# Causal mask folded into the bias rows, and row tiles taken from last to first

## The reference, cut to what matters

```python
s = jnp.einsum('bqhd,bkhd->bhqk', q_blk, k) * scale       # 128 query rows, 8 heads of 64
s = s + (F_blk[..., :, None] - Fh[..., None, :])          # the bias; Fh is a cumulative sum
s = jnp.where(kpos[None, :] <= qpos[:, None], s, NEG_INF) # the causal mask
p = jax.nn.softmax(s, axis=-1)
out = jnp.einsum('bhqk,bkhd->bqhd', p, v)
```

## Time and profile before

| | |
|---|---|
| median of 3 runs | 1316.46 us (1313.67 to 1316.74) |
| profiled execution | 1316.77 us |
| its span, first to last instruction | 1315.0 us |
| TensorE busy | 1287.6 us (98%) |
| VectorE / GpSimd / ScalarE busy | 698.0 / 610.7 / 401.7 us |
| mean granted TensorE clock | 0.996 |
| attention, slots 0 to 63 | from about 55.6 to 345 us |

### The profile page before, as it was taken

How to read it: one execution, slowest core, us unless ns; L and a number is a source line. 1 busy time by engine, 2 the same in 40 slices (tenths; PEclk the granted TensorE clock), 3 DMA queues, 4 the chain that set the end, 5 groups by cost and what they waited for, 6 DMA issues and landing times.

```text
span 1315.0 us, 20412 instructions
## 1 busy us (share of the span) xinstructions
PE 1287.6 (98%) x7189; PEld 1013.3 (77%) x7189; DVE 698.0 (53%) x1033; ACT 401.7 (31%) x590; POOL 610.7 (46%) x286
## 2 busy tenths in 40 slices
PE   8999999999999999999999999999999999999996
PEld 7988999998788777777777777777777777666675
DVE  5855656534657845547367473746545235312338
ACT  4646666664522241121212112020212102012016
POOL 1027878763301457475766757566662112021114
PEclk9999999999999999999999999999999999999999
DMA  7344545320362077776876868767674635577633
GB/s 246 124 152 138 171 158 175 124 89 1 128 236 78 31 232 289 245 244 230 285 254 213 270 223 273 239 229 264 236 259 155 202 129 184 219 258 270 251 118 129
DMA packets 111534, 254.96 MB, mean 194 GB/s; under 512 B 12624, under 2 KB 22737, under 8 KB 106048
## 3 DMA queue, kind: packets, MB, share of 16 engines
q1 hardware_dynamic: 66440, 181.96, 40.4%
q10 hardware_dynamic: 44032, 69.22, 15.7%
q0 software_dynamic: 960, 2.47, 0.5%
HBM read 243.72 MB, written 10.12 MB: 193 GB/s over the span
## 4 chain that ended last, share of the span: by engine, by line
PE 88%; DVE 6%; ACT 2%; issue 2%; DMA 1%; SPq 1%; POOL 0%; DVEq 0%; ACTq 0%; POOLq 0%
PE PSM L1574 35%; PE PSM L1584 16%; PE PSM L1298 12%; PE PSM L1410 5%; PE PSM L1634 4%; PE PSM L1311 3%; PE PSM L1377 3%; PE PSM L1361 2%; PE PSM L1680 2%; PE PSM L1553 1%; PE PSM L1693 1%; PE PSM L1332 1%; DVE ACC L2209 1%; DVE ACC L2228 1%; DMA QB<-q_d 1%
## 5 line engine op out<-in xcount | busy, mean ns | idle before, releaser
L893 POOL TENSOR_TENSOR WL<-WR,WH 128x1024 fp32r<-128x1024 f32 x55 | 132.0, 2400 | 379.6 <-ACT WH L1136 379.6
L801 POOL TENSOR_TENSOR AR<-AR,QB 128x1024 f32<-128x1024 f32 x96 | 238.4, 2503 | 55.0 <-DMA AR<-cache_k 52.2
L1574 PE MATMUL PSM<-XH,WH 128*128 128x512 f32 x672 | 213.5, 399 | 0.0
L1574 PE MATMUL PSM<-XL,WH 128*128 128x512 f32 x672 | 208.0, 391 | 0.0
L1574 PE MATMUL PSM<-XH,WL 128*128 128x512 f32 x672 | 207.1, 389 | 0.0
L2180 DVE TENSOR_TENSOR ACC<-ACC,PSM 128x512 f32<-128x512 f32 x160 | 108.4, 683 | 137.1 <-PE PSM L1584 136.9
L1136 ACT CAST WH<-WR 128x1024 fp32r<-128x1024 f32 x55 | 57.5, 1047 | 347.1 <-PE PSM L1574 179.4
L1574 PEld LDWEIGHTS PSM<-XH,WH 128*128 128x128 f32 x672 | 121.9, 188 | 50.4 <-issue 27.6
L1584 PE MATMUL PSM<-R 128*128 128x512 f32 x528 | 148.4, 390 | 0.1
L1574 PEld LDWEIGHTS PSM<-XH,WL 128*128 128x128 f32 x672 | 126.1, 188 | 27.4
L1574 PEld LDWEIGHTS PSM<-XL,WH 128*128 128x128 f32 x672 | 126.1, 188 | 27.3
(11 more groups left out here) (285 smaller groups left out, 2021.5 us busy)
## 6 DMA issues: line engine op xcount, KB each, us to landing
AR<-cache_v ACTq DMA_DIRECT2D x248, 256.0 KB, 4.2
AR<-cache_k SPq DMA_DIRECT2D x192, 256.0 KB, 4.0
AR<-ws SPq DMA_DIRECT2D x37, 1024.0 KB, 6.5
WR<-ffn SPq DMA_DIRECT2D x66, 512.0 KB, 4.6
WR<-w_in SPq DMA_DIRECT2D x20, 512.0 KB, 4.0
ACC<-cache_k SPq DMA_DIRECT2D x32, 256.0 KB, 2.8
WR<-cache_k SPq DMA_DIRECT2D x32, 256.0 KB, 3.1
WR<-w_o SPq DMA_DIRECT2D x5, 1024.0 KB, 5.3
```

What stands on the lines that cost most here:

```text
L801: pool.tensor_tensor(keys, keys, QB[:].rearrange("p (o n) -> p o n", o=1).to_broadcast([P, KP, AW]), ALU.mult).then_inc(k_mul, 1)
L893: pool.tensor_tensor(lo, WR[:, raw_weight(e), :], hi.bitcast(F32), ALU.subtract).then_inc(ffn_lo, 1)
L1574: ins = pe.matmul(out[:, hc], (hi, lo)[a][:, k * P:(k + 1) * P], x[b][:, k, hc], start=(k == 0 and n == 0), stop=(k == KC - 1 and n == 2))
```

## The change

The causal tile (zeros, and -1e30 above the diagonal) is no longer added by a product of TensorE in each of 64 score tiles. Instead it is added, in place, to block i of the bias row NF[hh] before row tile i is read. Block i then stays masked, and a row tile with a larger i would need it unmasked: so the row tiles of a head go from last (i = 7) to first (i = 0), by the new function `row_tile`. GpSimd adds the tile for slots 0 to 47 (`mask_block`, 48 instructions), VectorE for slots 48 to 63 (16 instructions). The addition for slot x+1 waits until VectorE has read slot x, and stands at the end of what GpSimd does in slot x; VectorE's instruction of slot x+1 waits for it (`masked`). The product steps are shared out evenly over the half slots. The mask has a tile of its own, and the rounded copies of identity and mask (two ScalarE instructions, `cons_hi`) are gone. `weighted_values` takes the tiles in their new order with the same number of products.

```diff
+POOLMASKS = STEPS * (PAIRS - 1)
+def row_tile(s):
+    return RT - 1 - s % RT
 def product_steps():
-    share = [RT + 4 - s % RT for s in range(STEPS) for _ in range(2)]
+    share = [1] * (2 * STEPS)
...
-            sp.wait_ge(cons_hi, 2)
...
+            def mask_block(x):
+                p, s = divmod(x, STEPS)
+                hh, i = s // RT, row_tile(s)
+                if s % RT == 0:
+                    pool.wait_ge(nf_ld[hh], 16 * (p + 1))
+                block = NF[hh][:, i * P:(i + 1) * P]
+                pool.tensor_tensor(block, block, causal[:], ALU.add).then_inc(masked, 1)
+                pool.wait_ge(masked, x + 1)
+
+            pool.wait_ge(small_ld, 16 * 7)
+            mask_block(0)
             for x, p, s in slots():
...
                 for n in range(EARLY):
                     if EMUL[n] == x:
                         multiply(n)
+                if x + 1 < POOLMASKS:
+                    pool.wait_ge(s_free, U["s", x] + 1)
+                    mask_block(x + 1)
...
-            act.copy(identR[:], ident[:]).then_inc(cons_hi, 1)
-            act.copy(causalR[:], causal).then_inc(cons_hi, 1)
...
             def scores(x, p, s):
-                hh, i = s // RT, s % RT
-                if i == 0:
+                hh, i = s // RT, row_tile(s)
+                if s % RT == 0:
...
                 for c in range(0, w, HALF):
                     n = min(HALF, w - c)
-                    diag = c + n == w
                     for part in (1, 2):
                         ins = pe.matmul(ps[:, c:c + n], R2[:, 3 * hh, i * P:(i + 1) * P],
-                                        R2[:, 3 * hh + part, c:c + n], start=(part == 1),
-                                        stop=(part == 2 and not diag))
-                    if diag:
-                        ins = pe.matmul(ps[:, w - P:w], identR[:], causalR[:], start=False, stop=True)
+                                        R2[:, 3 * hh + part, c:c + n], start=(part == 1), stop=(part == 2))
...
-                for kt in range(i + 2):
-                    for a in range(max(0, kt - i), 2):
+                for kt in range(i + 1):
+                    for a in range(2 if kt < i else 1):
...
                     dve.wait_ge(s_full, U["s", x] + 1)
-                    if i == 0:
-                        dve.wait_ge(nf_ld[hh], 16 * (p + 1))
+                    dve.wait_ge(masked, x + 1)
                     if x >= 2:
                         dve.wait_ge(tb_full, T["t", x - 2] + 1)
                     dve.tensor_tensor_reduce(L[x % 2][:, 0:w], S[:, 0:w], NF[hh][:, 0:w], -SCALE, 3e38,
                                              ALU.add, ALU.min, negm[:, x % 2:x % 2 + 1]).then_inc(s_free, 1)
+                if POOLMASKS <= x + 1 < SLOTS:
+                    q, r = divmod(x + 1, STEPS)
+                    dve.wait_ge(s_free, U["s", x] + 1)
+                    if r % RT == 0:
+                        dve.wait_ge(nf_ld[r // RT], 16 * (q + 1))
+                    block = NF[r // RT][:, row_tile(r) * P:(row_tile(r) + 1) * P]
+                    dve.tensor_tensor(block, block, causal[:], ALU.add).then_inc(masked, 1)
```

More of the change, by code:

```diff
@@ L249, in build @@
         ident = sb("ident_sb", [P, P])
-        identR = sb("identR", [P, P], F32R)
-        causalR = sb("causalR", [P, P], F32R)
+        causal = sb("causal_sb", [P, P])
         QB = sb("QB", [P, AW])
@@ L456, in build @@
         xswf_ld, small_ld, raw_ld = sem("xswf_ld"), sem("small_ld"), [sem(f"raw_ld{n}") for n in range(WS)]
-        consts, cons_hi = sem("consts"), sem("cons_hi")
+        consts, masked = sem("consts"), sem("masked")
         small_hi, small_lo = sem("small_hi"), sem("small_lo")
@@ L537, in _ @@
             for dst, src in ((bfc[:], t["bf"]), (cum, t["cum"]),
-                             (ident[:], t["ident"]), (causal, t["causal"]), (psc[:], t["pscale"]),
+                             (ident[:], t["ident"]), (causal[:], t["causal"]), (psc[:], t["pscale"]),
                              (page, t["page"]), (LNEW, t["newmask"])):
@@ L1055, in scale_row @@
             def scale_row(x):
-                w = (x % RT + 1) * P
+                w = (row_tile(x) + 1) * P
                 act.wait_ge(inv_done, x + 1)
@@ L1082, in _ @@
                 if 0 <= v < SLOTS and v % 2:
-                    w = (v % RT + 1) * P
+                    w = (row_tile(v) + 1) * P
                     act.wait_ge(tb_full, T["t", v] + 1)
@@ L1374, in weighted_values @@
                 pe.wait_ge(tb_free, T["vn", p] + 1)
-                for kt in range(i + 2):
-                    for a in range(max(0, kt - i), 2):
+                for kt in range(i + 1):
+                    for a in range(2 if kt < i else 1):
                         ins = pe.matmul(ob[HD * a:HD * a + HD, 0:P], VN[p % 2][:, kt * P + hh * HD:kt * P + hh * HD + HD],
-                                        PT[a][:, kt * P:(kt + 1) * P], start=(kt == 0), stop=(kt == i + a),
+                                        PT[a][:, kt * P:(kt + 1) * P], start=(kt == 0), stop=(kt == i - a),
                                         skip_group_check=True)
@@ L1454, in _ @@
                     pe.wait_ge(l_done, v + 1)
-                    turn(lambda i: L[v % 2][:, i * P:(i + 1) * P], n=v % RT + 1).then_inc(tb_full, 1)
+                    turn(lambda i: L[v % 2][:, i * P:(i + 1) * P], n=row_tile(v) + 1).then_inc(tb_full, 1)
                 if x in MIXSLOT:
@@ L1936, in _ @@
                     q, r = divmod(v, STEPS)
-                    hh, i = r // RT, r % RT
+                    hh, i = r // RT, row_tile(r)
                     dve.wait_ge(ob_full, O["pv", v // 2] + 1)
@@ L1946, in _ @@
                     for a in range(2):
-                        ins = dve.tensor_copy(pair_rows(q)[hh * HD:(hh + 1) * HD, (i + a) * P:(i + a + 1) * P],
+                        ins = dve.tensor_copy(pair_rows(q)[hh * HD:(hh + 1) * HD, (i - a) * P:(i - a + 1) * P],
                                               OB[a * HD:(a + 1) * HD, 0:P])
```

2 lines of the change are left out of this document (removed).

## The result

The changed kernel takes 1342.88 us (median of 5 runs, 1341.39 to 1345.29), the kernel before 1315.74 (5 runs beside them): ratio 1.0205, interval [1.0193, 1.0217]. It is slower, as predicted, but by 27 us and not by 12: the forecast was 1328.4 and its range ended at 1337. The sign held, and so did the time lost up to slot 16; the price of pairs 1 and 2 did not.

The account below looks back on a forecast made before the run. TensorE, busy 98% of the span, was taken as the bound. Terms: 1316.77 + 11.5 (slot 11 later) - 6.4 (mask products from slot 11) + 7.0 (pairs 1 and 2) - 0.5 (tail) = 1328.4 us; range 1317 to 1337.

Parts of the forecast that it names:

- the time lost up to slot 16: Start to slot 16: predicted 10.9 us longer, with the mask products of the stretch taken off.
- The mask products: 64 TensorE mask products removed: worth 0.12 us each, 7.7 us in all; bounds 3.8 and 15.0 us.
- Slots 0 to 2 and 8 to 11: Pair 0: scan 4.0 us later, then slot 9's addition behind multiplications awaiting QB; slot 11 starts at 120.5, +11.5 us.
- a sign of being right: TensorE idle 5 to 9 us near 105 to 118 us, with a low clock behind.
- Pairs 1 and 2: Waits for additions in slots 16 to 20 and 8 and 9 of the pair: 3.5 us per pair, 7 for two.
- The clock: Granted clock falls after TensorE waits: 1.6 us each time, counted as new only behind slots 9 and 10.
- rival C: Pairs 0 to 2: four waits each cost 1.6 us through the clock, additions take 1.2 us; 1336.8 us, chance 0.15.
- nearly all of the loss made before slot 36: Sign of being right: nearly all the lost time arises before slot 36.
- Pair 3 and the tail: Pair 3: VectorE adds the mask itself, costing nothing; tail: last tile 128 columns instead of 1024, -0.5 us (0 to -1.5).
- The cost of one addition: A 128-column mask addition on GpSimd: 0.5 us, with 0.25 and 1.2 kept as alternatives.
- GpSimd's time for wide two-input work: Trace read as milder than the skill: GpSimd 2.00 us against VectorE's 1.2 for a similar width.
- the reason I had kept 1 us for: GpSimd's first real instruction might need time to get ready: taken as 0, with 1 us kept.

## Why the prediction was wrong, point by point

By the runs, the time is made up so: 1316.6 - 4.6 (products gone) + 7.7 (order and share) + 7.6 (additions, even when they stand first) + 2.3 (place of slot 9's) + 13.1 (place in pairs 1 and 2) = 1342.7 us. The first three differences are successive and add up by construction; only the last two were measured apart, and they make 15.4 of the 15.6 us between the kernel with all additions first and the changed one. Each difference is uncertain by about 2 us.

**The mask products** were 0.12 us each in the sum and are 0.07. I took the distance between the starts in one slot less a product's usual one; the lower bound of 0.06, the distance to the next start, was the better value. 3.1 us of the miss (3.9 by the ratio).

**Slots 0 to 2 and 8 to 11** came out nearly in size, slot 11 at 118.69 for 120.5, with the chain of waits and the low clock as foretold; but partly by luck. Slot 0 started 1.9 us later than in the forecast, QB came 16.6 us behind slot 5's transposes (106.04 and 89.45) where I had 18.5, and TensorE waited 4.4 us in slots 9 to 11 (4.17 and 0.21) where I had nearly 9. Between 105 and 118 us it was busy 8.62 of 13.00, so idle 4.4: under the 5 to 9 us that I had named as a sign of being right. What I did not ask is how much of it is due to the wide tiles. With no addition at all slot 11's score instruction already comes 3.8 us late (114.00 to 110.20, 1.9 of them there at slot 0), since the late queries also hold slot 9 through VectorE's sum over keys; and with slot 9's addition first only 2.3 us come back.

**Pairs 1 and 2** are the step that failed. It read "Wait: about 1.5 us, and some 0.7 in slots 19 and 20" and "1.5 us" for slots 8 and 9 of the pair, 3.5 us a pair (the three terms make 3.7). The additions' place alone cost 13.1 us in the two pairs, where the sum had 7.0 for everything new there. Three things are missing in it:

- I followed the tile of slot 17 through its own chain and asked when TensorE wants it. The addition delays all that VectorE does behind it as well, and the copy of the values was there, with TB. TensorE waited 2.80 us in slot 17, before it came to the tile that I had priced.
- I took 4.5 us of TensorE's work against a chain of 5 in slots 22 to 25. In fact three additions in a row stand behind long instructions, and each may only start when VectorE has read the tile before: so slot 24 follows slot 23 at GpSimd's pitch of 5.2 us, and TensorE, with tiles of 256 and 128 columns there, waits 2.83 us for the buffer S.
- Slot 27 was not looked at: its addition stands behind a multiplication that waits for a key page. Moving it alone gave nothing; but a gain behind slot 22 appeared only when the additions of slots 25 to 31 were moved too.

**The clock** was left out for these waits in the forecast and put into rival C. Behind the waits of 2.8 us the granted clock falls to a mean of 0.70 and 0.58 in the next 4 us in slots 25 and 33, and to 0.79 over 256 to 264 us behind that of slot 41; each costs 1 to 2 us. The rival had four such falls at 1.6 us where there are three. It ended at 1336.8 because it kept 3.5 us a pair. The sign "nearly all of the loss made before slot 36" nearly came true (21.3 of 25.0 us), although the pairs' price was wrong.

**Pair 3 and the tail**: "nothing" was wrong by 3.2 us, mask products counted. Without any addition the new order takes 78.32 us from slot 48 to slot 63, where the kernel before without products takes 76.21: it is the order, 2.1 us. VectorE's 16 additions add 0.7, although they take it 0.89 us each, three times their own 0.29. These are differences of two profiles. The tail gave 1.1 us for the 0.5 foretold.

**The cost of one addition**, 0.46 us (the least and the median of 48 are 0.45 and 0.46), was right. GpSimd's time for wide two-input work was read too low: "milder, 2.00 us" took one row, but the multiplications of 1024 columns take 2.36 us each, 1.9 times VectorE's 1.23. It does not change the sum. One of the 48 took longer, and not for the reason I had kept 1 us for. The timeline, after, slots 0 to 2 (it answers to the earlier trace rows):

```profile
58.78 0.47 POOL L834 TENSOR_TENSOR AR<-AR,causal_sb 128x128 f32<-128x128 f32 x1
60.78 2.31 POOL L834 TENSOR_TENSOR AR<-AR,causal_sb 128x128 f32<-128x128 f32 x1 [1.52 <-DVE negm L1888]
...
59.40 1.22 DVE L1888 CUSTOM_DVE_ANT_0 AR<-PSM,AR 128x1024 f32<-128x1024 f32 x1 [2.47 <-POOL AR L834]
60.55 2.29 DVE L1872 TENSOR_TENSOR_SCAN ACC<-AR,ACC 128x1024 f32<-128x1024 f32 x1
```

The first real instruction takes 0.47 us. The second starts while VectorE's scan of two SBUF inputs runs, and ends 0.25 us behind it. Slot 0 starts at 59.40 where I had 57.55, but in the other kernels with the same front it started between 57.16 and 59.79, so 1 to 2 us of it are the execution's.

## What to carry to other kernels

A short instruction that another engine waits for can cost far more than its length, by what stands ahead of it in its queue: 48 additions of 0.46 us cost 23 us behind the slot's long work and 8 us ahead of it. To price it, follow not only the waiting instruction but everything behind it in its own queue, above all copies that free a shared buffer, and compare the pitch of the new queue (5.2 us from slot 23 to slot 24) with the least work that the bound engine has in any slot. When one wait on a late input is removed, look for the next one on the same input: here the sum over keys held slot 9 nearly as long as the addition had. And give a wait of a few us on the bound engine its clock: up to 2 us more each.

## What the runs showed of the hardware

**The same wait does not always lower the clock.** TensorE waited 2.8 us at the same instruction of slot 17 in three kernels that are alike up to there: the changed kernel, the one with slots 22 to 24 first, the one with slots 22 to 31 first. The timeline of TensorE of the first and the last of them, from the transposes behind the wait to the next scores, and for each the stretch from 152 us on:

```profile
150.11 1.09 PE L1325 MATMUL PSM<-ident_sb,AR 128*128 128x128 f32 x8 [2.80 <-DVE AR L1929]
152.48 0.86 PE L1373 MATMUL PSM<-R 128*128 128x512 f32 x4
```
```profile
152.00:156.00 4.00, 4.00 (x29) 3.89 (x28) 2.25 (x7) 3.04 (x5) 3.84 (x4) 1.00 0.02 4
```
```profile
151.34 1.97 PE L1328 MATMUL PSM<-ident_sb,AR 128*128 128x128 f32 x8 [2.79 <-DVE AR L1932]
155.75 1.48 PE L1376 MATMUL PSM<-R 128*128 128x512 f32 x4
```
```profile
152.00:156.00 4.00, 4.00 (x17) 4.00 (x16) 1.87 (x4) 0.89 (x2) 3.84 (x3) 0.50 0.02 4
```

From the transposes to the next scores it is 2.37 and 4.41 us, and 3.74 in the kernel between them (151.14 to 154.88, clock 0.59): the same idle time costs nothing more in one execution, 1.4 us in another and 2.0 in a third, by whether and how soon the clock goes to its lower level of 1.2 GHz (0.50). Two more kernels wait as long there: the one with slot 8 first shows 2.37 us and a clock of 1.00, the one with slots 26 and 42 first 4.41 us and 0.50. A forecast can give such a wait a mean, not a value.

**VectorE and GpSimd shut each other out** where VectorE's instruction has both inputs in SBUF: an addition of 0.29 us on VectorE takes up to 2.40 and ends 0.15 us behind GpSimd's instruction; the other way round there is one case, an addition of 0.46 us on GpSimd that takes 2.31 and ends 0.25 us behind VectorE's scan. Moving such work from one of the two engines to the other doesn't take it out of the other's way.
